# Sums of squares of the norms taken with tokens on partitions, between the last output products; root and reciprocal on 4 columns

## The reference

```python
def rmsnorm(x, g):
    xf = x.astype(jnp.float32)
    y = xf * lax.rsqrt(jnp.mean(xf * xf, axis=-1, keepdims=True) + EPS)
    return (y * g.astype(jnp.float32)).astype(x.dtype)

def modulated_norm(x, g, shift, scale):
    return rmsnorm(x, g) * (1 + scale) + shift

def swiglu(h, wg, wu, wd):
    return (jax.nn.silu(h @ wg) * (h @ wu)) @ wd
```

## Time and profile before

| | |
|---|---|
| median of three runs | 1776.3 us (1769.67 to 1780.38) |
| profiled execution, span | 1774.8 us |
| TensorE busy | 1652.7 us (93%), 13051 instructions |
| VectorE busy | 997.8 us (56%) |
| ScalarE busy | 783.6 us (44%) |
| old sums (L687) | 144 instructions, 37.7 us busy |
| root on 256 columns (L1314) | 9 of 15, 0.47 us each |
| reciprocal on 256 columns (L1707) | 9, 1.75 us each |
| granted TensorE clock, mean | 0.959 |

### The profile page before, as it was taken

One profiled execution on the slowest core, in us unless ns is written; L12 is line 12 of the kernel. 1 busy time (PEld: TensorE's weight loads), 2 busy tenths in 40 slices (PEclk: granted clock), 3 DMA queues, 4 the chain that ended last, 5 costly groups with the idle time before them and its releaser, 6 DMA issues.

```text
span 1774.8 us, 30505 instructions
## 1 busy us (share of the span) xinstructions
PE 1652.7 (93%) x13051; PEld 1539.7 (87%) x13051; DVE 997.8 (56%) x1044; ACT 783.6 (44%) x808; POOL 17.2 (1%) x24
## 2 busy tenths in 40 slices
PE   5999999789999999998998999999899889999995
PEld 3999988679999899998997999898788678989895
DVE  3444357655434544445655444555664568888883
ACT  2433345434333343334434334443454346766762
POOL 0000000300000000000000000000000000000000
PEclk7999999799999999999999999999999889999998
DMA  9767767434787657774534655444433529999990
GB/s 316 261 240 287 282 223 268 145 119 167 266 287 274 235 192 250 288 258 151 167 120 135 198 188 183 157 145 120 123 97 117 184 81 313 346 338 328 342 335 37
DMA packets 263921, 379.89 MB, mean 214 GB/s; under 512 B 12185, under 2 KB 223006, under 8 KB 263838
## 3 DMA queue, kind: packets, MB, share of 16 engines
q1 hardware_dynamic: 263838, 378.70, 63.2%
HBM read 377.63 MB, written 1.05 MB: 213 GB/s over the span
## 4 chain that ended last, share of the span: by engine, by line
PE 71%; DMA 10%; DVE 9%; ACT 5%; issue 3%; SPq 1%; DVEq 0%; ACTq 0%
PE ps L576 20%; PE ps L577 19%; PE ps L578 19%; DMA raw<-in_w_exp_up_dram 8%; PE ps L702 4%; DVE wlo L2165 3%; DVE wlo L1663 2%; ACT whi L1295 2%; ACT whi L1285 2%; PE ps L687 1%; DMA ada_raw<-in_w_ada_dram 1%; DVE rstd L1707 1%; SPq L497 1%; PE ps L1146 1%; DMA raw<-in_w_exp_down_dram 1%
## 5 line engine op out<-in xcount | busy, mean ns | idle before, releaser
L1663 DVE TENSOR_TENSOR wlo<-raw,whi 128x2048 fp32r<-128x2048 f32 (+1 forms) x191 | 433.0, 2268 | 526.2 <-ACT whi L1285 526.0
L576 PE MATMUL ps<-hhi,whi 128*128 128x256 f32 (+1 forms) x2024 | 587.1, 290 | 28.6 <-DVE hlo L1673 17.5
L577 PE MATMUL ps<-hlo,whi 128*128 128x256 f32 (+1 forms) x2024 | 578.5, 286 | 0.0
L578 PE MATMUL ps<-hhi,wlo 128*128 128x256 f32 (+1 forms) x2024 | 578.0, 286 | 0.0
L1285 ACT ACTIVATE whi<-raw 128x2048 fp32r<-128x2048 f32 (+1 forms) x191 | 360.3, 1887 | 345.2 <-DMA raw<-in_ffn_wd_dram 205.4
L576 PEld LDWEIGHTS ps<-hhi,whi 128*128 128x128 f32 (+1 forms) x2024 | 394.0, 195 | 36.1 <-issue 27.3
L577 PEld LDWEIGHTS ps<-hlo,whi 128*128 128x128 f32 (+1 forms) x2024 | 394.2, 195 | 1.8 <-issue 1.4
L578 PEld LDWEIGHTS ps<-hhi,wlo 128*128 128x128 f32 (+1 forms) x2024 | 393.9, 195 | 0.0
L576 PE MATMUL ps<-hidhi,whi 128*128 128x256 f32 x704 | 202.3, 287 | 2.0 <-DVE wlo L1768 2.0
L578 PE MATMUL ps<-hidhi,wlo 128*128 128x256 f32 x704 | 199.1, 283 | 0.0
L577 PE MATMUL ps<-hidlo,whi 128*128 128x256 f32 x704 | 199.0, 283 | 0.0
(11 more groups left out here) (271 smaller groups left out, 2374.2 us busy)
## 6 DMA issues: line engine op xcount, KB each, us to landing
ada_raw<-in_w_ada_dram SPq DMA_DIRECT2D x72, 1024.0 KB, 6.6
raw<-in_ffn_wg_dram SPq DMA_DIRECT2D x44, 1024.0 KB, 10.6
raw<-in_ffn_wu_dram SPq DMA_DIRECT2D x44, 1024.0 KB, 11.5
raw<-in_ffn_wd_dram SPq DMA_DIRECT2D x44, 1024.0 KB, 8.6
raw<-in_w_in_dram SPq DMA_DIRECT2D x18, 1024.0 KB, 5.4
raw<-in_w_exp_gate_dram SPq DMA_DIRECT2D x16, 1024.0 KB, 7.1
raw<-in_w_exp_up_dram SPq DMA_DIRECT2D x16, 1024.0 KB, 10.6
raw<-in_w_exp_down_dram SPq DMA_DIRECT2D x16, 1024.0 KB, 5.8
```

What stands on the lines that cost most here:

```text
L576: pe.matmul(o, wh, xh, start=start, stop=False, skip_group_check=shared)
L577: pe.matmul(o, wh, xl, start=False, stop=False, skip_group_check=shared)
L578: return pe.matmul(o, wl, xh, start=False, stop=stop, skip_group_check=shared)
L1663: dve.tensor_tensor(wlo[s][:, 0:width], raw[s][:, 0:width], whi[s][:, 0:width].bitcast(F32), ALU.subtract).then_inc(split[s], 1)
```

## The change

The sums are turned: the squared tile is now the stationary operand and two columns of ones are the moving one, so the sums of 128 tokens land on 128 partitions, in two equal columns. Two halves of the tokens give four columns of bank 7, accumulated over the eight tiles behind an opening product with zeros that clears them. The work is cut by pairs (`norm_pair`, four products each). In a feed-forward tail pair 0 goes before m = 5 and pair 1 before m = 7; after mix0, mix1 and blk2 pair 0 goes behind the third output unit and pair 1 behind the fourth; pairs 2 and 3 follow the last output product. A pair waits for the square of its own two tiles. In the first and the last norm all four pairs stand together.

Root and reciprocal are taken on 4 columns (`sums_ready`, `root_ready`, `rinv_ready`). `norm_spread` then multiplies each column of reciprocals, read as a [128,128] stationary operand by repeating it, with the identity: two products of 128 columns that put the reciprocal of every token on all partitions, in the upper half of bank 7. The scaled tiles read it there, in PSUM, instead of in `rstd`. Bank 7 is free again only when all eight scaled tiles are made, so the router's logits move to bank 5. In the first norm the spread stands behind the first vector's turn.

```diff
--- before.py
+++ after.py
@@ -193,6 +193,7 @@
         bada = sb("bada", [P, 2 * NMOD * KT])
         modv = sb("modv", [P, 2 * NMOD * KT])
         adarow = sb("adarow", [P, T])
+        rinv = sb("rinv", [P, 4])
         cact = sb("cact", [P, KT])
         gmod = sb("gmod", [P, KT])
         ghalf = sb("ghalf", [P, KT])
@@ -677,16 +678,34 @@
 
             norms = [0]
 
-            def norm_sums():
-                norms[0] += 1
-                counts["x_ready"] = 4 * norms[0]
-                own(7)
-                for k in range(KT):
-                    if k % 2 == 0:
-                        wait("sq_ready")
-                    mm = pe.matmul(ps[:, 7, 0:T], ones, hf[:, k, :], start=(k == 0), stop=(k == KT - 1))
-                mm.then_inc(sem("stat_ready"), 1)
-                frees(7, "stat_read")
+            def norm_pair(pr):
+
+                if pr == 0:
+                    own(7)
+                    pe.matmul(ps[:, 7, 0:4], zeros[:, :], zeros[:, 0:4], start=True, stop=True)
+                wait("sq_ready")
+                for k in (2 * pr, 2 * pr + 1):
+                    for t in range(2):
+                        mm = pe.matmul(ps[:, 7, 2 * t:2 * t + 2], hf[:, k, t * P:(t + 1) * P], ones[:, 0:2], start=False,
+                                       stop=(k == KT - 1), skip_group_check=True)
+                if pr == 3:
+                    mm.then_inc(sem("sums_ready"), 1)
+                    norms[0] += 1
+                    counts["x_ready"] = 4 * norms[0]
+
+            def norm_spread():
+
+                wait("rinv_ready")
+                for t in range(2):
+                    mm = pe.matmul(ps[:, 7, T + t * P:T + (t + 1) * P], rinv[:, 2 * t:2 * t + 1].to_broadcast([P, P]), ident,
+                                   start=True, stop=True)
+                mm.then_inc(sem("rstd_ready"), 1)
+                freed[7] = (sem("t_ready"), KT * norms[0])
+
+            def norm_sums(pairs=range(4)):
+                for pr in pairs:
+                    norm_pair(pr)
+                norm_spread()
 
 
             def ada_quarter(r, n, v_before=None):
@@ -723,9 +742,12 @@
             wait("cact_ready")
             ada_half(0, 0)
             pe.wait_ge(sem("lam_exp"), 1)
-            norm_sums()
+            wait("zeros_ready")
+            for pr in range(4):
+                norm_pair(pr)
             ada_half(0, 1)
             ada_turn(0)
+            norm_spread()
             ada_vector(1)
             ada_turn(1)
 
@@ -765,6 +787,8 @@
                     for m in range(KT):
                         if last and m == 4:
                             pe.wait_ge(split[2], c + b0[2] + 1)
+                        if last and m in (5, 7):
+                            norm_pair((m - 5) // 2)
                         o = ps[:, 2 + m // 2, (m % 2) * T:(m % 2 + 1) * T]
                         for k in range(2):
                             mm = three(o, wh[:, k, m * P:(m + 1) * P], wl[:, k, m * P:(m + 1) * P],
@@ -809,10 +833,10 @@
                     with pe.Fori(nv, pairs) as i:
                         pair(i)
                 down(count - 1, (count - 1) % 2, last=True)
+                norm_sums((2, 3))
                 for s in range(3):
                     turn[s] = b0[s] + count
 
-            wait("zeros_ready")
             chunked("ffn0", 2)
 
 
@@ -945,27 +968,25 @@
                 frees(b, "x_ready")
             for u in (10, 11):
                 linear("mix0", u, "x_ready", mhi, mlo)
+                norm_pair(u - 10)
 
             def outputs(stage, u0, ready=None):
                 for j in range(4):
                     linear(stage, u0 + j, "x_ready", mhi, mlo, ready if j == 0 else None)
-
-            norm_sums()
+                    if j > 1:
+                        norm_pair(j - 2)
+
+            norm_sums((2, 3))
             chunked("ffn1", 9)
-            norm_sums()
             chunked("ffn2", 14, 4)
 
 
-            norm_sums()
             first_units(("evacuated", "v_done"))
             for u in range(2, 12):
                 linear("mix1", u, ("evacuated", "v_done", "y_done")[u % 3])
             outputs("mix1", 12, lambda k: wait("mix_split") if k % 2 == 0 else None)
-            norm_sums()
+            norm_sums((2, 3))
             chunked("ffn3")
-
-
-            norm_sums()
 
             def rope(r):
 
@@ -1109,19 +1130,19 @@
                         frees(2 + u % 2, "x_ready")
             for u in (30, 31):
                 linear("blk2", u, "x_ready", b=2 + u % 2)
-
-
-
-            norm_sums()
-            own(7)
-            pe.matmul(ps[0:NG + NE, 7, 0:T], brout[:, :], ones[0:1, 0:1].to_broadcast([1, T]), start=True, stop=False)
+                norm_pair(u - 30)
+
+
+
+            norm_sums((2, 3))
+            pe.matmul(ps[0:NG + NE, 5, 0:T], brout[:, :], ones[0:1, 0:1].to_broadcast([1, T]), start=True, stop=False)
             for k in range(KT):
                 pe.wait_ge(sem("t_ready"), 7 * KT + k + 1)
                 for t in range(2):
                     mm = pe.transpose(ps[:, 2 * t + k // 4, (k % 4) * P:(k % 4 + 1) * P], hf[:, k, t * P:(t + 1) * P], ident)
                 if k % 4 == 3:
                     mm.then_inc(sem("h_turned"), 1)
-                mm = pe.matmul(ps[0:NG + NE, 7, 0:T], wrout[:, k, :], hf[:, k, :], start=False, stop=(k == KT - 1))
+                mm = pe.matmul(ps[0:NG + NE, 5, 0:T], wrout[:, k, :], hf[:, k, :], start=False, stop=(k == KT - 1))
             mm.then_inc(sem("logits_ready"), 1)
             wait("logits_copied")
             for t in range(2):
@@ -1306,7 +1327,8 @@
                         refill(slots[pr])
                     wait("x_ready")
                     act.activation(hf[:, 2 * pr:2 * pr + 2, :], xT[:, 2 * pr:2 * pr + 2, :], ACT.Square).then_inc(sem("sq_ready"), 1)
-                roots(D, T)
+                wait("sums_ready")
+                act.activation(root[:, 0:4], ps[:, 7, 0:4], ACT.Sqrt, bias=eps[:, 0:1], scale=1.0 / D).then_inc(sem("root_ready"), 1)
 
             def roots(width, n, b=7, o=0):
 
@@ -1703,8 +1725,8 @@
                                   bada[:, sl].rearrange("p (j b) -> p j b", j=4), ALU.add).then_inc(sem("mod_ready"), 1)
 
             def root_inverse():
-                wait("stat_read")
-                link(dve.reciprocal(rstd[:, 0:T], root[:, 0:T]))
+                wait("root_ready")
+                dve.reciprocal(rinv[:, :], root[:, 0:4]).then_inc(sem("rinv_ready"), 1)
 
             root_inverse()
             refill(0)
@@ -1725,9 +1747,10 @@
                     root_inverse()
                 if slot is not None:
                     refill(slot)
+                wait("rstd_ready")
 
                 def scaled(k):
-                    stt(hf[:, k, :], xT[:, k, :], gain[:, k:k + 1], rstd[:, 0:T], ALU.mult, ALU.mult).then_inc(sem("t_ready"), 1)
+                    stt(hf[:, k, :], xT[:, k, :], gain[:, k:k + 1], ps[:, 7, T:2 * T], ALU.mult, ALU.mult).then_inc(sem("t_ready"), 1)
 
                 def low(k):
                     wait("h_high")
@@ -2079,7 +2102,7 @@
 
             htok_low(0)
             wait("logits_ready")
-            dve.tensor_copy(adarow[0:NG + NE, :], ps[0:NG + NE, 7, 0:T]).then_inc(sem("logits_copied"), 1)
+            dve.tensor_copy(adarow[0:NG + NE, :], ps[0:NG + NE, 5, 0:T]).then_inc(sem("logits_copied"), 1)
             wait("logits_turned")
             link(dve.tensor_copy(logit[:, :, :], ps[:, 6, 0:P].rearrange("p (t n) -> p t n", t=2)[:, :, 0:NG + NE]))
             rank = c_("rank")
```

## The result

The changed kernel takes 1783.3 us (median of 16 runs, 1775.8 to 1787.5), beside 1777.5 (16 runs, 1769.7 to 1782.0) for the kernel before on the same chips: the ratio is 1.0042, 95% interval 1.0026 to 1.0058 (the two medians alone give 1.0033). That is slower by +5.8 us between the medians. The interval lies wholly above 1, and the ratio is a little under the 0.5% from which the prediction counts a change. The profiled execution's span is 1781.7 us, beside 1774.8.

What follows compares the result with a forecast made beforehand. TensorE carries 71% of the chain, and a norm costs the time its big products stand still. Norms -0.5, clock +1.5 and next stages' starts +3.7 give +4.7 us: median 1776.3 becomes 1781, range 1766 to 1790.

Steps and rivals of the forecast that it cites:

- Price of a narrow instruction: Sums with 2 columns: 0.113 us an instruction at full clock, 0.215 at half; 0.90 a pair, as before.
- rival (c): Narrow products cost only 0.45 us a pair, so tails and final norm gain: 1769 us, chance 0.08.
- Root, reciprocal, spread: Between last sum and first scaled tile: root 0.2, reciprocal 0.16, spread 0.75 with handovers; 1.2 us in all.
- Feed-forward tails: Norm tails: +0.33 us each after ffn0 and ffn1, -0.07 after ffn2 and ffn3, plus 0.3 each for the clock.
- rival (a): The clock falls inside each tail before the last pair: +11.4 us, 1787.7, chance 0.17.
- mix0's tail: Norm after mix0: pairs 1 and 2 hide the last square, scaled tile 0.95 us earlier; 0.3 added for the clock.
- mix1: Norm after mix1: -0.3 us, as the refill waits for ScalarE's copy and the reciprocal's 1.59 is lost.
- blk2 and the final norm: Norm after blk2 -0.8 us at low clock; final norm +0.15, its longer sums nearly offset.
- Norm 1: First norm: clock at half, a quarter of w_ada takes 1.94 us instead of 1.07: +0.87.
- Starts of the next stages: First products after norms: zeros behind the spread cost +1.8 us after ffn1; half of 3.8, +1.9, after mix0; +3.7 together.
- The slow start stays as it is: Next stage's start after ffn0, already slow with about 2 us lost, was taken as unchanged by the change.
- Rival (b): The clock stays up, so five slow starts of some 1.6 us vanish: -12.4 us, 1764, chance 0.10.

Runs made afterwards that it cites:

- kernel 3: The changed kernel, still 2 columns, with all four pairs behind m=7 in the four feed-forward tails: 1779.9 us, 1.0029 to the kernel before.
- kernel 2: The changed kernel with 128 columns of ones instead of 2 in all nine norms: 1766.7 us, 0.9947 to the kernel before.
- kernel 1: The changed kernel with 128 columns of ones instead of 2 in norm 1 alone: 1782.1 us, 1.0034 to the kernel before.
- kernel 8: The changed kernel with 128 columns of ones in norms 2 to 9 and 2 in norm 1: 1768.5 us, 0.9957 to the kernel before.
- kernel 9: The kernel before, norms untouched, with unread 256-column products behind the sums of six norms: 1767.3 us, 0.9954 to the kernel before.
- kernel 5: The changed kernel with 128 columns in all norms and all pairs behind m=7 in feed-forward tails: 1764.1 us, 0.9930 to the kernel before.

## Why the prediction was right, and where its steps were not

The prediction said +4.7 us, from the median then known of 1776.3 to 1781; measured are +5.8 between the medians of sixteen runs each. The sign and the size hold, and so does the mechanism in the main: the gain in root and reciprocal is eaten by the placing of the pairs, and the clock makes the rest. Where the clock's cost falls was forecast less well. Step by step:

- **Price of a narrow instruction**: forecast 0.113 at full clock and 0.215 at half. Measured 0.116 (3.71/32, kernel 3) and 0.218 (6.97/32). Right; rival (c), cheap narrow products, falls. The Trainium skill, "TensorE: Matmul & The Clock Gate", section "Back-to-back issue gap", gives about 60 cycles, 25 ns, for so few columns, but as the gap of a matmul without the time of its weight load, and it says that in a stream of weight loads and matmuls both set the spacing. Here every sum instruction has a weight load of its own, so the 25 ns could not be carried over; the traces show 0.116 us.
- **Root, reciprocal, spread**: forecast 0.2, 0.16 and 0.65 (0.75 with two handovers); measured 0.263, 0.178 and 0.71 (1.22 at half clock). Last sum to first tile: 270.44 - 269.05 = 1.39 us, forecast 1.2. The scaled tiles that read PSUM take 0.87, as the additions of the earlier trace rows: free, as costed.
- **The stall ahead of m=5**: seen after ffn0 (0.33 us) and ffn1 (0.34), none after ffn2 or ffn3, as worked out.
- **Feed-forward tails**: forecast +0.33 plus 0.3 for the clock after ffn0 and ffn1; measured +0.59 and +0.80. After ffn2 +0.09 against -0.07 and 0.3. After ffn3 +1.41 in place of the same: there rival (a) came true in one tail. The window 1154 to 1155 of the changed kernel has the clock at 0.91, those behind it, until 1165, 0.50, and the last pair and the spread pay (timeline of the changed kernel):

```profile
1155.30 1.87 PE L689 MATMUL ps<-cst,hf 128*128 128x2 f32 x8 [0.84 <-ACT hf L1329]
1157.21 0.26 ACT L1331 ACTIVATE root<-ps,lam 128x4 f32<-128x4 f32 x1 [1.96 <-PE ps L689]
1157.74 1.22 PE L700 MATMUL ps<-cst,rinv 128*128 128x128 f32 x4 [0.57 <-DVE rinv L1729]
```

- **mix0's tail**: forecast -0.95 with 0.3 for the clock; measured -0.83.
- **mix1**: from pair 3's square to the first scaled tile forecast -0.3, measured -0.02. The last pair fell to half clock (eight instructions in 1.39 us; kernel 2, at full clock, shows -0.26), a cost that I had left out of this norm. The refill starts on ScalarE's copy, as forecast, at 951.06 + 1.90 (timeline of the changed kernel):

```profile
951.06 1.90 ACT L1306 ACTIVATE whi<-raw 128x2048 fp32r<-128x2048 f32 x1
...
952.99 2.29 DVE L1685 TENSOR_TENSOR wlo<-raw,whi 128x2048 fp32r<-128x2048 f32 x1 [1.55 <-ACT whi L1306]
```

- **blk2 and the final norm**: last square to first tile -0.7 after blk2 (forecast -0.8), and +0.10 at the end (forecast +0.15). Right.
- **Norm 1**: forecast +0.87, one slow quarter of w_ada. In the profile it is +3.4 (+0.15 to +3.55): I charged the quarter, but not the sums themselves, which took 6.97 us at half clock beside 4.01 before. Over many runs kernels 1 and 8 put it at 1.4 to 1.8, within their intervals. The mechanism shows in this trace, not in every one (kernel 3 has the same sums nearly all at full clock); the term was too small, by some half to one us if these medians are right.
- **Starts of the next stages**: forecast +1.9 after mix0 and +1.8 after ffn1. After mix0 the clock fell in the middle of the zeros, for 3.4 us, so that they took 2.67 us beside 2.09 before, and it cost +1.0 to the 96th product (+3.14 to +4.13); in kernels 1 and 3, whose norm there is the same, it fell for 6.8 us and cost 2.5. The forecast, half of 3.8, lies between. After ffn1 the mechanism is there in full: the zeros take 3.65 us at half clock and the first product comes 1.37 us later than the tile does (+6.31 against +4.94), but at the 96th product the offset is +5.20, so only 0.3 of it is left. The starts that I had left at nothing moved by -0.2 after ffn0, +0.9 after ffn2, -0.6 after mix1 and +0.55 after ffn3. All starts together: +1.9 where +3.7 was forecast. Timeline of the changed kernel after mix0 and after ffn1:

```profile
399.37 2.67 PE L804 MATMUL ps<-zeros 128*128 128x128 f32 x16
...
621.99 0.93 PE L700 MATMUL ps<-cst,rinv 128*128 128x128 f32 x4 [0.64 <-DVE rinv L1729]
622.58 3.65 PE L804 MATMUL ps<-zeros 128*128 128x128 f32 x16
622.97 0.87 DVE L1695 SCALAR_TENSOR_TENSOR hf<-xT,gmod,ps 128x256 f32<-128x256 f32 x2 [1.03 <-PE ps L700]
```

- **The experts' stage**: not in the prediction at all, and +2.1 in the trace, from the first scaled tile of norm 8 to pair 0's square of norm 9. From 1500 to 1700 both kernels load at the same pace (DMA share 1.01 to 1.02, 334 to 340 GB/s), so the stage is held by its loads, and between 1450 and 1460 they ran at 107 GB/s in the changed kernel, at 190 before. I took that for the reason. But kernel 1, which is the changed kernel in that stage, shows 107 GB/s in the same window and loses nothing (-0.3), and over all traces the stage moves by -2.9 to +2.1. So the +2.1 belong to this execution, and no cost of the change is shown there.
- **"The slow start stays as it is"**: this was the sentence with the most in it, and the weakest. I took the half clock after each norm as given and priced only how the change would add to it. Experiments 2 and 9 show that it is not given: it was worth 8 us in the kernel before, and its release is what the change could have brought. Rival (b), "the clock stays up", said 1764 at a chance of 0.10. As a forecast of this kernel it was wrong; kernel 5, which differs from it by the width and the place of the pairs, runs in 1764.1. Its largest term was right: five slow starts at 1.6, 8 us in all, where kernel 9's trace gives 8.2. That the two totals are so near is partly luck: its 3 us for norm 9 did not come (from the last square to the first tile -0.3 in kernel 5, +0.8 in kernel 2).
- **Sums of the prediction**: the terms of (c) as listed add up to 11.3 us, not 12, so 1770 rather than 1769. With the 25 ns of the skill three pairs on a tail's path would gain 0.7 us each, an estimate of 2.1 us a tail and not 1.5. Neither changes the forecast.

So the total was right partly by luck, with errors that offset: norm 1 and ffn3's tail too cheap, the starts after mix0 and ffn1 too dear, and 2.1 us of the experts' stage that the next execution need not have. What stays open is how far the single profiled execution stands for the median, norm by norm. Norm 1 and the experts' stage show that it can be off by 2 us.

## What to carry to other kernels

Count a TensorE instruction not only by its time but by whether it keeps the clock: where a reduction with `ones` is made narrow to save columns, more columns cost little (a pair's eight instructions took 0.95 to 1.06 us with 2 columns and 1.05 to 1.16 with 128, both at full clock) and can hold the clock for what follows. Before a stage that starts slowly, look at the granted clock in the windows around its first products; if it is 0.50 behind a gap in which TensorE waits for a short chain on the other engines, unread wide products in the gap are a cheap trial (8 us here). And when a chain is shortened, look at what was hidden under it: work that lay under a reciprocal of 1.75 us has no cover under one of 0.18.

## What the runs showed of the hardware

- Around norms 2 to 7 the granted clock was at 0.50 for 44 to 58 us in the traces with sums of 2 and 32 columns, 34 with 64, and 3 to 14 with 128, for the same number of products. Whole-kernel ratios by width: 2 columns 1.0042, 32 columns 1.0056, 64 columns 1.0017, 128 columns 0.9947. TensorE is busy for 94% of the span with 2 columns and with 128, so the busy share on the page does not show the difference.
- With a weight load of 128x128 f32 ahead of each, an instruction of 2 columns costs 0.12 to 0.13 us at full clock and one of 128 columns 0.13 to 0.145 (a pair's time by eight): nearly the same. In an unbroken row of 32 it is 0.116 with 2 columns. At 0.50 it is 0.218 with 2.
- A reciprocal on VectorE takes 1753 ns on 256 columns and 178 on 4, which is what turning the data gains; a root on ScalarE takes 263 ns on 4 columns and 470 on 256.
